# The mLSTM's four projections as seven half-size products instead of eight

## The chip, the cores and the metric

The kernel runs on one NeuronCore of a Trainium2 chip. The metric is the device time of one execution in microseconds (us); lower is better. TensorE (PE) multiplies, VectorE (DVE), ScalarE (ACT) and GpSimd (POOL) do the elementwise work, SyncE (SP) issues most transfers.

## The reference, cut to what matters

A two-layer hybrid encoder step on 256 prompt and 64 sample frames, 320 columns in all, in 32-bit floats, model width 1024. Each layer is

```
h = rms(x, norm_mix)
proj = h @ w_in            # among its columns m_q, m_k, m_v, m_o, 256 wide each, and m_if, 8 wide
y_a: conv + RG-LRU   y_b: latent attention   y_c: retention   y_d: mLSTM(m_q, m_k / 8, m_v, gates from m_if)
x = x + concat(head_rms(y_a), head_rms(y_b), head_rms(y_c), head_rms(y_d) * sigmoid(m_o)) @ w_out
x = x + (silu(g) * u) @ w_down,   g, u = rms(x) @ w_gu
```

The mLSTM part first needs the two gate rows for each head (a running sum of log-sigmoid and a running maximum over the frames), then q, k and v.

## The kernel before

All activations stand transposed in on-chip memory: `hT` is the normalised input, 8 tiles of 128 features by 320 frames. A layer runs through stages whose order is written out by hand, engine by engine, in four functions (`tensor`, `scalar`, `vector`, `gpsimd`); semaphores tie them together. `need(engine, name, ...)` waits for a named result, `step` issues an instruction that announces one (and waits for it on its own engine), `claim(pe, use)` waits until the last user of a PSUM bank has been read, `fill` announces that a bank is full. `layer_uses` lists which of the 8 banks each use has, in order. PE takes its instructions strictly in the order written, so a wait at one of them holds back all that follow.

Weights come in chunks of 256 columns (1 MB) through a ring of 5 slots, loaded by SP in the order ql, kvr, mo, mv, mq, mk, rq and so on; a slot is loaded again when PE has used its last chunk. 

The stage of the change lies between the products of the latent keys (`kvr`, line 891) and the first mLSTM scores (`ds0`, lines 813 to 815). On PE it is: `mo` (two outputs of 128 features, 8 products of 128x128 by 320 columns each, line 785), four transposes of the old state (layer 0 alone, line 901), the gates' transposes `mgt` (907), `mv` (785), `cnT`, `qms` (915, 920), the transposes of the values `mvt0`, `mvt1` (797), the latent queries `qt0` to `qt2` (927), `mq` and `mk` (785), three tiles of attention keys `kv0` to `kv2` (860), the gate rows' transposes `rT` and `gx` (948, 954), the first retention query `rq0` (785), the mLSTM keys' transposes `mkt` (806), and `ds0`. An instruction on 32-bit data shows as two in the profile, so one projection is 32 rows of line 785.

On DVE the stage is a long chain in one order: latent queries (1705, 1706), key copies (1698, 1701), latent sum, then from 1730 the latent keys with their norm (to 1744), the clamp of `mo` (1749), gate rows (1753 to 1757), rotary keys (1760 to 1770), in layer 0 a state table (1683) and the decay-rate table `lam_tables` (1659 to 1677, in the middle of which it waits for an exponential of ACT, line 1384), `lfr` (1776), the copies of the latent queries (1782), the scans and five row operations on 4 partitions (1788 to 1795), the queries' norm and rotation (1800 to 1823), the copies of `mq` (1807), and the key copies of `kv0` to `kv2`. ACT copies `mv` and `mk` out of PSUM (1387, 1416), makes the keys' squares (1354), then the sigmoid of the output gate (1306 to 1308), and copies `gx` (1429), the bank of which `ds0` takes over. POOL only issues transfers in this stage.

The feed-forward part already uses a seven-product form (Strassen's, in Winograd's variant): a 2x2 block product of weight quarters by halves of the 320 columns takes 7 products of 160 columns instead of 8 (line 1133). POOL makes three sums of weight quarters for each chunk (lines 602 to 605, four instructions of 128x512), DVE adds the products up (2104 to 2112).

Of the kernel before, what the change touches and what calls it, by code (L numbers as in the profile page):

```python
# [21 lines left out]
P = 128  # L22
# [39 lines left out]
NQ = KT // 2  # L62
MIXES = FT - 1 + 3 * NQ
MSLOTS = 3
# [60 lines left out]
def layer_uses():  # L125
# [9 lines left out]
    d("ql0", "ql1", "kvr", "mo0", "mo1", "mgt", "mv0", "mv1")  # L135
    u += [("cnT", (4,)), ("qms", (5,))]
    d("mvt0", "mvt1")
    u += [("qt0", (6,)), ("qt1", (7,)), ("qt2", (2,))]
    d("mq0", "mq1", "mk0", "mk1")
# [52 lines left out]
LAST_USE = {"kvr": "kvr", "ql": "ql1", "mo": "mo1", "mv": "mv1", "mq": "mq1", "mk": "mk1", "rq": "rq1",  # L192
# [6 lines left out]
def build(nc, I, O):  # L199
    with ExitStack() as ctx:  # L200
# [120 lines left out]
        gate = part(2, T)  # L321
        dmx = part(512)
        dh = part(2, 512)
        wt = part(2, 576)
        vw = part(2, NT, HD + 1)
        qg = part(H, P)
        ytm = part(NT, H, HD)
# [7 lines left out]
        xgm = mixT  # L335
        dhf = dh[:, :, :].rearrange("p a n -> p (a n)")
# [248 lines left out]
        def _(pool):  # L585
            step = stepper(pool, "pool_chain")

            def mix_weights(l, i):
# [8 lines left out]
                if i == 1:  # L597
                    need(pool, "h_sums", l, 4)
# [27 lines left out]
            for l in range(DEPTH):  # L626

                if l == 0:
# [15 lines left out]
                    pool.dma_start(cst[:, c1:], I["consts"][:, c1:]).then_inc(sem("tables_loaded"), 16)  # L644
                need(pool, "ckv_new", l, 1)
# [4 lines left out]
                out(O["s_krope"][l, 0], krr[0:DEC, 2, :])  # L650
                need(pool, "m_rows", l, 1)
# [5 lines left out]
                out(O["s_mm"][l].rearrange("b h -> h b"), mro[:, T - 1:T])  # L657
                need(pool, "q_ready", l, 1)
# [70 lines left out]
        def _(pe):  # L729
# [58 lines left out]

            def value_tiles(which, l, p):
# [3 lines left out]
                need(pe, "v_raw", l, 4, (0 if which == "mv" else 2) + p + 1)  # L793
# [60 lines left out]
            for l in range(DEPTH):  # L854
# [39 lines left out]
                for p in range(2):  # L894
                    feature(f"mo{p}", l, "mo", p * P, P)
                if l == 0:
# [6 lines left out]
                    ins.then_inc(sem("rows_turned"), 1)  # L903
                claim(pe, "mgt", l)
# [4 lines left out]
                for p in range(2):  # L909
                    feature(f"mv{p}", l, "mv", p * P, P)  # L910
# [11 lines left out]
                for p in range(2):  # L922
                    value_tiles("mv", l, p)
                for t in range(NT):
# [4 lines left out]
                    fill(ins, f"qt{t}")  # L929
                if l == 0:  # L930
# [3 lines left out]
                for p in range(2):  # L934
                    feature(f"mq{p}", l, "mq", p * P, P)
                for p in range(2):
                    feature(f"mk{p}", l, "mk", p * P, P)
# [5 lines left out]
                if l == 0:  # L943
                    pe.wait_ge(sem("ct_ready"), 1)
# [14 lines left out]
                need(pe, "mq_ready", l, 2)  # L959
# [163 lines left out]
                def product(use, l, i, p, right, opens, closes):  # L1123
# [3 lines left out]
                    if p in (3, 5, 6, 7):  # L1127
                        need(pe, "mixed", l, MIXES, i + 1)
# [36 lines left out]
                def hidden_units(j):  # L1165
# [11 lines left out]
                    def h_sum(n, made_n):  # L1177
                        def right(k):
                            if j == 1 and k == 0:
                                need(pe, "h_sums", l, 4, made_n)  # L1180
# [104 lines left out]
        def _(act):  # L1285
# [49 lines left out]
            for l in range(DEPTH):  # L1335
# [40 lines left out]

                if l == 0:
# [4 lines left out]
                if l == 0:  # L1382
                    act.wait_ge(sem("lam"), 1)
                    A(lamt[:, 1, :], lamt[:, 0, :], ACT.Exp, scale=-1.0).then_inc(sem("lam_exp"), 1)
# [12 lines left out]
                for p in range(2):  # L1397
                    value_raw(f"mv{p}", p)
# [5 lines left out]
                for p in range(2):  # L1404
                    value_copy("mv", "d", p)
# [3 lines left out]
                       qtm[:, :, :, :].rearrange("p t h e -> p (t h e)"), ACT.Square), "q_stats")  # L1409
                need(act, "q_ms", l, 1)  # L1410
# [798 lines left out]
```

## Time and profile before

| | |
|---|---|
| median of 3 runs | 928.33 us (928.27 to 928.68) |
| the profiled execution's own time | 928.3 us |
| its span, first to last instruction | 926.5 us |
| PE, DVE, ACT, POOL busy | 920.3, 498.6, 209.9, 444.4 us |
| granted TensorE clock, mean | 1.000 |

The profile is that of one execution. Busy time of PE includes modelled ends of matmuls, so near 100% says that there was always one in flight, not that it went at its peak. The time lies 1.8 us above the span.

### The profile page before, as it was taken

Reading aid. Unit: us, or ns where it says so; the run is one execution under the profiler, and the core shown is the slowest. Engines: PE = TensorE matmul, PEld = TensorE weight load, DVE = VectorE, ACT = ScalarE, POOL = GpSimd, SP = SyncE. Lnnn points to the kernel's source line nnn. Section 1 sums busy time; section 2 is a strip of 40 time slices with the busy share of each in tenths; the row PEclk is TensorE's granted clock in tenths of the full one; section 3 lists DMA queues with packets and bytes.
Section 4 is the critical chain, followed back from the end, with each engine's and each line's share of the span. In section 5 each row is a group of like instructions: output and inputs, shape, how many; then the busy total and the mean of one; then the engine's idle time right before and its main releaser. Section 6 shows DMA issues by size and latency. Waiting matters only on the chain.

```text
span 926.5 us, 14897 instructions
## 1 busy us (share of the span) xinstructions
PE 920.3 (99%) x5712; PEld 812.7 (88%) x5712; DVE 498.6 (54%) x1018; ACT 209.9 (23%) x457; POOL 444.4 (48%) x469
## 2 busy tenths in 40 slices
PE   8999999999999999999999999999999999999998
PEld 6777877778999999999977678777799999999998
DVE  6674656845565656512363665577356556563221
ACT  3224255432000000100132244462310011100001
POOL 6210380125966666676411215403268666666670
PEclk9999999999999999999999999999999999999999
DMA  9969312129555554433434673112655555533321
GB/s 280 237 131 98 112 46 92 52 17 251 138 139 141 142 141 144 134 129 126 133 124 136 30 147 96 47 48 50 138 150 141 143 142 143 147 125 126 131 94 39
DMA packets 159636, 113.02 MB, mean 122 GB/s; under 512 B 10247, under 2 KB 157357, under 8 KB 159437
## 3 DMA queue, kind: packets, MB, share of 16 engines
q1 hardware_dynamic: 154660, 104.50, 39.0%
q0 software_dynamic: 4272, 6.80, 7.3%
q8 instruction: 46, 0.75, 0.3%
q10 hardware_dynamic: 632, 0.75, 0.3%
q14 instruction: 26, 0.21, 0.1%
HBM read 108.46 MB, written 2.27 MB: 120 GB/s over the span
## 4 chain that ended last, share of the span: by engine, by line
PE 98%; DMA 1%; ACT 0%; SPq 0%; DVE 0%; issue 0%; DVEq 0%; ACTq 0%
PE ps L1133 52%; PE ps L785 20%; PE ps L1090 8%; PE ps L1151 2%; PE ps L891 1%; PE ps L860 1%; PE ps L987 1%; PE ps L927 1%; PE ps L1028 1%; PE ps L1037 1%; PE ps L813 1%; PE ps L833 1%; PE ps L970 1%; DMA arena<-in_x_sample 1%; PE ps L1048 1%; PE ps L1069 0%
## 5 line engine op out<-in xcount | busy, mean ns | idle before, releaser
L785 PE MATMUL ps<-hT,ring 128*128 128x320 f32 x608 | 169.4, 434 | 0.3 <-DVEq L433 0.3
L602 POOL TENSOR_TENSOR work<-ring 128x512 f32<-128x512 f32 (+1 forms) x66 | 81.8, 1239 | 153.7 <-issue 113.4
L785 PEld LDWEIGHTS ps<-hT,ring 128*128 128x128 f32 x608 | 113.7, 190 | 45.6 <-DVEq L433 0.8
L1133 PE MATMUL ps<-mixT,ring 128*128 128x160 f32 x672 | 105.0, 299 | 0.0
L1133 PE MATMUL ps<-hT,work 128*128 128x160 f32 x672 | 98.5, 299 | 0.0
L1133 PE MATMUL ps<-hT,ring 128*128 128x160 f32 x672 | 98.1, 299 | 0.0
L1133 PEld LDWEIGHTS ps<-mixT,ring 128*128 128x128 f32 x672 | 95.8, 190 | 0.0
L1133 PEld LDWEIGHTS ps<-hT,ring 128*128 128x128 f32 x672 | 93.7, 190 | 0.3
L1133 PEld LDWEIGHTS ps<-hT,work 128*128 128x128 f32 x672 | 93.7, 190 | 0.0
L604 POOL TENSOR_TENSOR work<-ring 128x512 f32<-128x512 f32 (+1 forms) x66 | 82.4, 1248 | 5.2
L603 POOL TENSOR_TENSOR ring<-ring 128x512 f32<-128x512 f32 (+1 forms) x66 | 82.2, 1246 | 5.2
L605 POOL TENSOR_TENSOR work<-ring,work 128x512 f32<-128x512 f32 (+1 forms) x66 | 81.9, 1242 | 5.2
L1562 ACT ACTIVATE arena<-ps 128x160 f32<-128x160 f32 x42 | 12.8, 304 | 286.8 <-PE ps L1133 286.8
L1090 PE MATMUL ps<-mixT,ring 128*128 128x320 f32 x256 | 71.1, 434 | 0.0
L2142 DVE TENSOR_TENSOR arena<-arena,ps 128x160 f32<-128x160 f32 x8 | 2.6, 321 | 118.6 <-ACT arena L1580 118.6
L1090 PEld LDWEIGHTS ps<-mixT,ring 128*128 128x128 f32 x256 | 48.0, 190 | 19.3
L1133 PE MATMUL ps<-work,ring 128*128 128x160 f32 x352 | 55.6, 299 | 0.0
L1133 PE MATMUL ps<-mixT,work 128*128 128x160 f32 x336 | 52.5, 299 | 0.0
L1133 PE MATMUL ps<-arena,work 128*128 128x160 f32 x352 | 51.7, 299 | 0.0
L1133 PEld LDWEIGHTS ps<-work,ring 128*128 128x128 f32 x352 | 50.4, 190 | 0.0
L1133 PEld LDWEIGHTS ps<-arena,work 128*128 128x128 f32 x352 | 49.1, 190 | 0.0
L1133 PE MATMUL ps<-arena,ring 128*128 128x160 f32 x330 | 48.7, 299 | 0.0
(398 smaller groups left out, 1389.9 us busy)
## 6 DMA issues: line engine op xcount, KB each, us to landing
ring<-in_w_gu SPq DMA_DIRECT2D x88, 512.0 KB, 5.2
ring<-in_w_in SPq DMA_DIRECT2D x44, 512.0 KB, 7.2
ring<-in_w_down SPq DMA_DIRECT2D x32, 512.0 KB, 4.4
ring<-in_w_out SPq DMA_DIRECT2D x16, 512.0 KB, 4.4
ring<-in_w_down SPq DMA_DIRECT2D x16, 384.0 KB, 3.4
cst<-in_consts POOLq DMA_DIRECT2D x1, 1664.0 KB, 12.2
ring<-in_w_in SPq DMA_DIRECT2D x2, 640.0 KB, 5.5
arena<-r POOLq DMA_DIRECT2D x8, 160.0 KB, 17.4
```

Source lines behind the costliest of these rows:

```text
L602: step(tt(s3, a11, a21, ALU.subtract))
L603: step(tt(a21, a21, a22, ALU.add))
L604: step(tt(s2, a21, a11, ALU.subtract))
L605: step(tt(s4, a12, s2, ALU.subtract), "mixed")
L785: ins = mm(bank(use, 0, T, m), w[:, k, c:c + m], right[:, k, 0:T], start=(k == 0), stop=(k == KT - 1))
L813: mm(bank(use, 0, 256), k[:, 0:128], q[:, 0:256], start=True, stop=True)
L833: ins = mm(bank(use, 200 + 64 * s, 64, e), a, b_, start=(t == tiles[0]), stop=(t == tiles[-1]))
L860: fill(mm(bank(f"kv{i}", 0, 512), lat, wkvb[:, :], start=True, stop=True), f"kv{i}")
L1090: ins = mm(bank(u, 0, T), w[:, k, (n % 2) * P:(n % 2 + 1) * P], mixT[:, k, :], start=(k == 6), stop=(k == 5), skip_group_check=True)
L1133: ins = mm(bank(use, at * HT, HT), left, right(k), start=(opens and k == 0 and at == 0), stop=(closes and k == n - 1), skip_group_check=True)
L1151: return mm(bank(use, 0, T), w[:, k, q * P:(q + 1) * P], xg[:, k, :], start=(k == 0), stop=(k == KT - 1))
L1562: step(A(p1c[:, j % 2, :], bank(f"fa{j}", 0, HT), ACT.Copy), "p1_copied")
```

## The change

Each of the four projections mo, mv, mq, mk becomes one `feature_pair` of seven products of 4 x (128x128 by 160 columns). Products that need only raw weights come first (1, 2, 4), then those with sums. Four half sums of `hT` are made once a layer by DVE (`half_sums`, after the latent queries), three sums of weight quarters for each projection by POOL (`pair_weights`, four instructions of 128x512), ACT copies the first product (`pair_first`), DVE combines the rest (`pair_result`, five instructions, for mo a clamp more). The results go to on-chip memory; ACT then copies queries and keys to their places. In DVE's order the scans move ahead of the copies of the latent queries, `state_tables` ahead of mo's result, and `lam_tables` behind mq's result. In PE's order the latent queries move ahead of the values' transposes, which now wait for mv's result. On POOL the sums stand among its transfers: mo and mv first, mq behind the four transfers of the latent keys, mk behind the broadcasts of the gate rows.

```
+    u += [("moa", (2,)), ("mob", (6,)), ("moc", (1,)), ("mgt", (0,)), ("mva", (5,)), ("mvb", (7,)), ("mvc", (4,))]
+    u += [("cnT", (6,)), ("qms", (0,)), ("qt0", (1,)), ("qt1", (2,)), ("qt2", (6,)), ("mvt0", (5,)), ("mvt1", (7,))]
+    u += [("mqa", (4,)), ("mqb", (0,)), ("mqc", (3,)), ("mka", (1,)), ("mkb", (2,)), ("mkc", (7,))]
 ...
     u += [("rT", (3,)), ("gx", (2,)), ("mkt", (6, 7))]
 # gpsimd
+            def pair_weights(l, i):
+                s2, s3, s4 = (pair_sums[i % 2][:, s] for s in range(3))
+                if i < 2:
+                    wait_filled(pool, ("ql1", "kvr")[i], l)
+                    if l == 0 and i == 1:
+                        pool.wait_ge(sem("rows_turned"), 3)
+                else:
+                    wait_used(pool, PAIRS[i - 2], l)
+                wait_chunk(pool, name, l)
+                step(tt(s3, a11, a21, ALU.subtract))
+                step(tt(a21, a21, a22, ALU.add))
+                step(tt(s2, a21, a11, ALU.subtract))
+                step(tt(s4, a12, s2, ALU.subtract), "mixed")
...
+                for i in range(2):
+                    pair_weights(l, i)
                 need(pool, "ckv_new", l, 1)
 ...
                 out(O["s_krope"][l, 0], krr[0:DEC, 2, :])
+                pair_weights(l, 2)
                 need(pool, "m_rows", l, 1)
 ...
                 out(O["s_mm"][l].rearrange("b h -> h b"), mro[:, T - 1:T])
+                pair_weights(l, 3)
                 need(pool, "q_ready", l, 1)
 # tensor
+            def feature_pair(name, l):
 ...
+                claim(pe, a, l)
+                one(a, 0, lambda k: w[:, k, 0, 0, :], half(0, 0), True)
+                one(a, 2, lambda k: w[:, k, 1, 0, :], half(1, 0))
+                claim(pe, c, l)
+                one(c, 1, lambda k: w[:, k, 1, 1, :], half_sum(4), True)
+                claim(pe, b_, l)
+                need(pe, "mixed", l, MADE, i + 1)
+                one(b_, 0, lambda k: w[:, k, 0, 1, :], half_sum(1), True)
+                fill(one(b_, 1, lambda k: s3[:, k, :], half_sum(2)), b_)
+                fill(one(a, 1, lambda k: s2[:, k, :], half_sum(3)), a)
+                fill(one(c, 0, lambda k: s4[:, k, :], half(1, 1)), c)
 ...
-                for p in range(2):
-                    feature(f"mo{p}", l, "mo", p * P, P)
+                feature_pair("mo", l)      # and so for mv, mq, mk
 ...
-                need(pe, "v_raw", l, 4, ...)
+                    need(pe, "pair_made", l, NPAIR, 2)      # value_tiles("mv")
 # scalar
+                def pair_first(name):
+                    if i > 0:
+                        need(act, "pair_made", l, NPAIR, i)
+                    wait_filled(act, f"{name}a", l)
+                    step(A(pair_p1, bank(f"{name}a", 0, HT), ACT.Copy), "p1_copied")
 ...
+                pair_first("mq")
+                need(act, "pair_made", l, NPAIR, 3)
+                for n in range(4):
+                    step(A(qh[rs, n, :], raw[rs, n // 2, :], ACT.Copy), "mq_ready")
+                pair_first("mk")
+                if l == 0:
+                    act.wait_ge(sem("lam"), 1)
+                    A(lamt[:, 1, :], lamt[:, 0, :], ACT.Exp, scale=-1.0).then_inc(sem("lam_exp"), 1)
+                key_stats(range(3), KTILES - 3)
+                need(act, "pair_made", l, NPAIR, 4)
                 for p in range(2):
+                    step(A(kf[:, p, 0:T], raw[:, 2 + p, :], ACT.Copy, scale=0.125), "mk_ready")
 # vector
+                def half_sums():
+                    step(v.tensor_tensor(hp[:, 0], h_at(0, 1), h_at(0, 0), ALU.subtract), "h_sums")
+                    step(v.tensor_tensor(hp[:, 1], h_at(1, 1), h_at(0, 1), ALU.subtract), "h_sums")
+                    step(v.tensor_tensor(hp[:, 2], h_at(1, 1), hp[:, 0], ALU.subtract), "h_sums")
+                    step(v.tensor_tensor(hp[:, 3], h_at(1, 0), hp[:, 2], ALU.subtract), "h_sums")
+                def pair_result(name):
+                    need(dve, "p1_copied", l, P1S, PAIRS.index(name) + 1)
+                    step(v.tensor_tensor(u2, p1, bank(a, HT, HT), ALU.add))
+                    step(v.tensor_tensor(c11, p1, bank(a, 2 * HT, HT), ALU.add), bank_read=(a, l))
+                    wait_filled(dve, b_, l)
+                    step(v.tensor_tensor(halves(u34), halves(bank(b_, 0, T)), u2..., ALU.add))
+                    step(v.tensor_tensor(c22, u34[:, HT:T], bank(b_, 0, HT), ALU.add), bank_read=(b_, l))
+                    wait_filled(dve, c, l)
+                    step(v.tensor_tensor(mid, halves(u34), halves(bank(c, 0, T)), ALU.add), "pair_made")
+                    # mo: then max(SIG_MIN) over 128x640, "pair_made"
 ...
                 query_latents(1)
+                half_sums()
 ...
+                if l == 0:
+                    state_tables()
+                pair_result("mo")
 ...
-                if l == 0:
-                    state_tables()
-                    lam_tables()
 ...
+                scans()
+                pair_result("mv")
                 need(dve, "qlat_rstd", l, 1)     # then the copies of the latent queries
 ...
+                pair_result("mq")
+                if l == 0:
+                    lam_tables()
+                pair_result("mk")
                 key_copies(range(3), KTILES - 3)
```

## Rows read from the trace of the kernel before

**Rows 1.** The page's first part: busy us, share of the span, instructions.
```profile
PE 920.3 (99%) x5712; PEld 812.7 (88%) x5712; DVE 498.6 (54%) x1018; ACT 209.9 (23%) x457; POOL 444.4 (48%) x469
```
**Rows 2.** The chain that ended last, in order: start us, us, what.
```profile
33.58 8.61 PE ps L785 x32
...
52.61 0.71 PE ps L797 x6
...
57.20 17.23 PE ps L785 x64
...
77.68 0.50 PE ps L954 x4
...
83.34 0.43 PE ps L813 x2
...
223.10 237.71 PE ps L1133 x1750
...
487.53 8.63 PE ps L785 x32
...
537.28 0.43 PE ps L813 x2
```
**Rows 3.** The DVE timeline: start us, us, engine, line, operation, tiles, shapes, count.
```profile
25.43 0.55 DVE L1706 SCALAR_TENSOR_TENSOR arena<-ps,cols,rstd 128x320 f32<-128x320 f32 x1
...
33.69 0.18 DVE L1730 COPY mift<-ps 128x24 f32<-128x24 f32 x1 [0.62 <-PE ps L891]
...
38.15 0.56 DVE L1744 TENSOR_TENSOR arena<-arena,bcn 128x384 f32<-128x384 f32 x1
...
58.07 0.68 DVE L1788 TENSOR_TENSOR_SCAN work<-cst,work 4x256 f32<-4x256 f32 x1
...
61.74 0.31 DVE L1795 TENSOR_SCALAR nm<-mro 4x320 f32<-4x320 f32 x1
...
76.23 0.42 DVE L1698 COPY arena<-ps 128x256 f32<-128x256 f32 x1 [4.92 <-ACT arena L1354]
...
221.99 0.83 DVE L2084 TENSOR_TENSOR mixT<-hT 128x640 f32<-128x640 f32 x1 [0.18 <-DVE hT L2077]
...
484.29 0.55 DVE L1706 SCALAR_TENSOR_TENSOR arena<-ps,cols,rstd 128x320 f32<-128x320 f32 x1
```
**Rows 4.** DVE's groups by line and form, 223 to 400 us: busy, mean ns, idle.
```profile
L2125 DVE TENSOR_TENSOR arena<-arena 128x160 f32<-128x160 f32 x11 | 14.1, 1282 | 0.4
...
L2107 DVE TENSOR_TENSOR arena<-ps,arena 128x320 f32<-128x320 f32 x21 | 10.3, 492 | 11.4 <-PE ps L1133 11.0
...
L2105 DVE TENSOR_TENSOR arena<-arena,ps 128x160 f32<-128x160 f32 x21 | 6.7, 321 | 0.8
```
**Rows 5.** POOL's groups by line and form, whole span.
```profile
L602 POOL TENSOR_TENSOR work<-ring 128x512 f32<-128x512 f32 x58 | 73.8, 1272 | 146.8 <-issue 108.8 <-DMA ring<-in_w_gu 21.5 <-DVE mixT L2087 15.9
```
**Rows 6.** The POOL timeline: four copies on 32 partitions, twice.
```profile
569.67 2.14 POOL L674 COPY work<-work 32x320 f32<-32x320 f32 x4 [1.29 <-DMA out_s_mn<-sst]
...
576.24 1.98 POOL L674 COPY work<-work 32x320 f32<-32x320 f32 x4
```
**Rows 7.** The POOL timeline around the stage of layer 0: its transfers.
```profile
27.52 0.66 POOL L644 DMA_DIRECT2D cst<-in_consts  x1
...
46.77 0.73 POOL L613 DMA_DIRECT2D out_p_krope<-arena  x1 [6.48 <-DVE arena L1770]
```
**Rows 8.** The DVE timeline: the decay-rate table after its wait, first and last.
```profile
47.81 0.23 DVE L1665 TENSOR_SCALAR lamt<-lamt 128x4 f32<-128x4 f32 x1
...
52.43 0.17 DVE L1677 TENSOR_SCALAR c<-lamt 128x4 f32<-128x4 f32 x1
```
**Rows 9.** The ACT timeline, 74 to 83 us.
```profile
74.46 0.44 ACT L1416 ACTIVATE work<-ps 128x320 f32<-128x320 f32 x1 [3.80 <-PE ps L785]
...
82.51 0.28 ACT L1429 ACTIVATE glb<-ps 128x132 f32<-128x132 f32 x1
```
**Rows 10.** The PE timeline: 24 products of 128 columns, the first of the execution.
```profile
1.07 4.92 PE L738 MATMUL ps<-work 128*128 128x128 f32 x24 [1.07 <-DVE work L1595]
```

More of the change, by code:

```diff
@@ L62 @@
 NQ = KT // 2
+PAIRS = ("mo", "mv", "mq", "mk")
+NPAIR = len(PAIRS)
 MIXES = FT - 1 + 3 * NQ
+MADE = NPAIR + MIXES
+P1S = NPAIR + FT - 1 + NQ
 MSLOTS = 3
@@ L326, in build @@
         qg = part(H, P)
+        ytm_at = wk
         ytm = part(NT, H, HD)
@@ L787, in feature, with one, half, half_sum @@
                     fill(ins, use)
+            def feature_pair(name, l):
+                i = PAIRS.index(name)
+                w, _ = quarters(name, l)
+                s2, s3, s4 = (pair_sums[i % 2][:, s] for s in range(3))
+                a, b_, c = f"{name}a", f"{name}b", f"{name}c"
+                def one(use, at, left, right, opens=False):
+                    for k in range(KT // 2):
+                        ins = mm(bank(use, at * HT, HT), left(k), right(k), start=(opens and k == 0),
+                                 stop=(k == KT // 2 - 1), skip_group_check=True)
+                    return ins
+                def half(jj, t):
+                    return lambda k: hT[:, 2 * k + jj, t * HT:(t + 1) * HT]
+                def half_sum(n):
+                    if i == 0:
+                        need(pe, "h_sums", l, 8, n)
+                    return lambda k: hp[:, n - 1, k, :]
+                wait_chunk(pe, name, l)
+                claim(pe, a, l)
[9 more added lines that the diff above has]
+                fill(one(c, 0, lambda k: s4[:, k, :], half(1, 1)), c)
             def value_tiles(which, l, p):
@@ L792, in value_tiles @@
                 claim(pe, u, l)
-                need(pe, "v_raw", l, 4, (0 if which == "mv" else 2) + p + 1)
+                if which == "mv":
+                    need(pe, "pair_made", l, NPAIR, 2)
+                else:
+                    need(pe, "v_raw", l, 2, p + 1)
                 if which == "rv":
@@ L908, in _ @@
                 fill(ins, "mgt")
-                for p in range(2):
-                    feature(f"mv{p}", l, "mv", p * P, P)
+                feature_pair("mv", l)
                 claim(pe, "cnT", l)
@@ L921, in _ @@
                 fill(ins, "qms")
-                for p in range(2):
-                    value_tiles("mv", l, p)
                 for t in range(NT):
@@ L929, in _ @@
                     fill(ins, f"qt{t}")
+                for p in range(2):
+                    value_tiles("mv", l, p)
                 if l == 0:
@@ L933, in _ @@
                     pe.wait_ge(sem("consts_loaded"), 16 * 5)
[L934 to L937, printed above, removed]
+                    pe.wait_ge(sem("ct_ready"), 1)
+                feature_pair("mq", l)
+                feature_pair("mk", l)
                 need(pe, "ckvT", l, 1)
@@ L1395, in value_copy @@
                     now_read(act, u)
-                for p in range(2):
-                    value_raw(f"mv{p}", p)
+                pair_first("mv")
                 wait_filled(act, "cnT", l)
@@ L1409, in _ @@
                        qtm[:, :, :, :].rearrange("p t h e -> p (t h e)"), ACT.Square), "q_stats")
+                for p in range(2):
+                    value_copy("mv", "d", p)
                 need(act, "q_ms", l, 1)
@@ L1745, in _ @@
                                      bcn[:, l, 0:KVR].unsqueeze(1).broadcast_to([P, NT, KVR]), ALU.mult), "ckv_new")
-                for p in range(2):
-                    wait_filled(dve, f"mo{p}", l)
-                    step(v.tensor_scalar(gate[:, p, :], bank(f"mo{p}", 0, T), SIG_MIN, None, ALU.max), "gate_arg")
-                    now_read(dve, f"mo{p}")
+                if l == 0:
+                    state_tables()
+                pair_result("mo")
                 wait_filled(dve, "mgt", l)
```

99 lines of the change are left out of this document (56 added, 43 removed).

## The prediction

> **What bounds the kernel now.** I read the page's busy times first: PE is busy in all but 6 us of the span, POOL and DVE in about half of it [rows 1]. Then the chain that ended last, in order of time: in the stage of the change it is PE alone, from one group to the next without a gap [rows 2]. So here a microsecond less of PE work is a microsecond gained, but only if every result that PE asks for is there in time; the timelines of DVE and POOL say how much room there is [rows 3, 7]. The page's share of busy time hides this: DVE looks half idle over the span, while in this stage it works nearly without pause.
>
> **What PE saves.** The pair mq and mk takes 17.23 us as 64 rows, so a projection 8.62 us. In the feed-forward part 1750 rows of 160 columns take 237.71 us, 0.1358 us each [rows 2]. Seven products of four matmuls are 56 rows: 7.61 us. That is 1.01 us for each of eight projections, 8.1 us together, if PE never waits. Nothing else on PE grows: the other groups stay, in another order.
>
> **What DVE gets.** By kind: a difference over 128x640 takes 0.83 us [rows 3], a sum with one operand in PSUM 0.32 us for 160 columns and 0.49 us for 320 [rows 4]. With the 0.03 us between instructions, the half sums are 3.4 us, a projection's result 0.32 + 0.32 + 0.49 + 0.32 + 0.49 = 1.94, with gaps 2.1 us, and mo's clamp over 640 elements at most 0.8. What they replace (the clamp and the copies out of PSUM, 0.5 us each for 320 columns) is about as long, so DVE's list grows by the half sums and little more; but now PE waits at the middle of it: the transposes of the values come only after the last instruction of mv's result, and ahead of that stand the whole of mo's result, the gate rows, the rotary keys and the scans.
>
> **POOL beside DVE, where I part from the plain sum.** In the feed-forward part a DVE difference of 128x160 with both operands in on-chip memory takes 1.28 us on average, the same size with one operand in PSUM 0.32 [rows 4]. POOL's weight sums take 1.27 us each at that time [rows 5]. So a DVE instruction that reads two operands from on-chip memory stands until the POOL instruction in flight ends: 0.96 us more each. PSUM operands free it from this. It doesn't depend on the number of partitions, on POOL's side at least: four copies on 32 partitions took 2.14 us beside DVE's work and 1.98 otherwise [rows 6]. The Trainium skill (SBUF — State Buffer, Who interferes with whom) has the same rule, a DVE instruction with two SBUF inputs against a GpSimd one that reads SBUF, as an exclusive lock held for a whole instruction; the trace agrees. Without that rule the sum below would end 13 us lower, before any loss by the clock. POOL had only transfers to issue in this stage [rows 7]; now it gets 4 x 1.27 us and gaps, 5.4 us, four times a layer.
>
> **DVE's chain, layer 0.** The last latent query ends at 25.98 [rows 3]. Half sums to 29.4; POOL's last early transfer ends at 28.2 [rows 7], mo's sums follow at once, so one half sum is held: 30.3. The key copies of the four past tiles, waiting on ACT in turn, took 26.83 to 32.09, so they end at 35.3; the latent sum, one operation held by POOL, at 37.2. The latent keys' work, which began at 33.69 because PE was done then [rows 3], begins 3.5 us later; one of its squares meets mv's sums (0.96), so its end, before at 38.71, is at 43.1. Then state table 0.7, mo's result 2.1 and clamp 0.8: 46.8; three gate rows 1.6; seven rotary operations 1.85; lfr 0.5: 50.8. The nine scans and row operations take 58.07 to 62.05, 4.0 us [rows 3]. POOL takes mq's sums 1.4 us after the rotary keys (two transfers of which the first takes 0.73 [rows 7]), so they fall on the scans: four of the nine are held, by 3.9 us. Scans end at 58.7, mv's result at 60.8. PE would be there much earlier: between 33.58 and 57.20 it has 23.6 us, less 0.7 for the six transposes [rows 2], less 2 x 1.01: at 54.4. It stands for 6.4 us.
>
> From there: transposes 0.7, mq and mk 15.2, then the 8.9 us that lie between 74.43 and ds0 at 83.34 [rows 2]: ds0 at 85.7 without another wait. Two more come in layer 0. DVE begins the decay-rate table ahead of mk's result, but the exponential that it waits for stands on ACT behind the copy of mk's first product, at 76.3. From there its 4.8 us [rows 8] and the four operations that read mk's bank, 1.6 us, end at 82.8; gx, 3.1 us behind mk's end at 76.8, wants that bank: 3.0 us. And ds0 waits for ACT to read gx: from DVE's first key copy to that read it took 76.23 to 82.79 [rows 3, 9], 6.6 us, now with the two key copies of 0.44 [rows 9], moved ahead of the sigmoid, and their gaps 7.5. The first copy is at 83.3, so ds0 at 90.8, another 2.1 us. Against 83.34 layer 0 loses 7.4 us.
>
> **Layer 1.** Half sums begin at 484.84 [rows 3], with POOL on mo's sums from 480.8: held twice, 490.1. The latent sum, held 0.6, ends at 491.6, where PE was done at 487.5 + 0.1; one held square, then as above without tables: latent keys 497.5, mo 500.5, gate rows 502.1, rotary keys 503.9, lfr 504.5, scans and 3.9 us held 512.4, mv's result 514.5. PE would be there at 507.9: 6.6 us. No table stands ahead of mk's result, so gx does not wait; ds0 follows at 514.5 + 0.7 + 15.2 + 8.9 = 539.3, and ACT's longer list adds 0.3: 539.7 against 537.28 [rows 2], 2.4 us lost. Both together 9.9 us. Behind ds0 DVE, ACT and PE keep their distances, PE is the bound again, and nothing is given back.
>
> POOL itself is in time: mo's sums end at 34.2 and are wanted at 37.3, mq's end 8 us and mk's 6 us ahead. I cost them at nothing. If POOL were late by more, PE would wait in the middle of a projection instead.
>
> **The clock.** PE never paused for over 1.3 us after its start. Its first 24 products of 128 columns, after a pause of 1.07 us and whatever came before, take 4.92 us, 0.205 each [rows 10]; by 0.1358 for 160 columns they would take about 0.109 each, an estimate, 2.6 us in all. The level of 1.2 GHz is my reading of the factor of 1.9. After a pause of 6.5 us the bounds are nothing and another such stretch, 2.3 us lost. I take the upper end for each layer, since a start after no work at all is the nearest row: 4.6 us. The Trainium skill (TensorE: Matmul & The Clock Gate, HAM oscillation — how this bites in real kernels) warns of falls of the clock in PE's pauses; no pause of the kernel before is long enough to show it.
>
> **The sum.** 928.3 us is the profiled execution's own time, within 0.03 of the median. 928.3 + 7.4 + 2.4 + 4.6 = 942.8, about 942.7 us.
>
> **Rivals.**
> 1. As above but the clock stays up: 928.3 + 9.9 = 938.2. The pauses may be too short, and the column of the granted clock shows full speed even in the slow first stretch, so the trace can't decide.
> 2. Scans and operations on 4 partitions are not held by POOL: no row shows either beside POOL's work. Then 3.9 us fall away in each layer, the rest being held or hidden: layer 0 loses 5.0, layer 1 gains 0.2: 933.1. The clock would stay up after pauses of 4 us, or cost up to 4 more.
> 3. Faster: nothing on DVE is held in this stage, since POOL's reads and DVE's here fall in different memory or the waits interleave better. The place is the values' transposes; mv's result would end at 53.9 and 507.4, where PE needs it at 54.4 and 507.9. It decides at 0.5 us of delay, from which on every microsecond is lost. Layer 1 gains 4.2, layer 0 still loses 0.9 by the two waits at mk: 925.0. Rows 4 speak strongly against it.
> 4. POOL is held so much by DVE that it is late for the products, or the clock stays down through the waits at mk in layer 0: 946 or more.
>
> **Chances and range.** Forecast 0.45, rival 1 0.22, rival 2 0.15, rival 3 0.10, the rest 0.08. Range 931.5 to 945.5, which leaves out rival 3 and the dearest cases. Faster, same and slower are parted at 0.2% (1.9 us), about what a measurement tells from no change. Faster 0.10, same 0.04 (a mixture of rivals 2 and 3 near 928), slower 0.86.
>
> **What the profile after would show.** PE: 56 rows for a projection in 7.6 us; a pause of some 6 us before the values' transposes (line 797's form with `work`) in each layer, ended by DVE; in layer 0 alone 3 us before gx and 2 us before ds0. DVE: four scans or row operations at 1.2 to 1.5 us instead of 0.3 to 0.5, half sums partly at 1.8. The granted clock below 1 behind the pauses. Wrong I am if the scans keep their lengths beside POOL's sums, if POOL's sums of mq come after the scans, or if the clock does not fall.

## The result, and the profile after

The changed kernel takes 946.13 us (median of 4 runs, 945.49 to 947.39), the kernel before 928.50 beside it: 1.0189 times as long, with a 95% interval of 1.0172 to 1.0207. The profiled execution took 945.51 us, its span 943.7. The forecast was 942.7 with a range up to 945.5. The sign and the hold came as forecast; the loss was put 3.4 us too low, and the measured time lies 0.6 us above the range. The trace explains 2.8 of the 3.4 us, since the profiled execution was 0.6 us faster than the median. Of all the executions below one stands apart, at 1363.86 us and a granted clock of 0.654 (one of ten without POOL's sums); the intervals leave it out.

The waits of PE, in the changed kernel (what waited, for whom; us in total, times, the longest). Before, PE had no such wait in either of these stages [rows 2]:

```profile
PE ps L872 <- DVE work L1823: 12.7, 2, 7.5
PE ps L1022 <- DVE work L1817: 3.0, 1, 3.0
PE ps L836 <- DVE mixT L1798: 1.9, 1, 1.9
PE ps L888 <- ACTq L448: 0.6, 1, 0.6
```

L872 are the transposes of the values, which wait in each layer for the last instruction of mv's result (L1823). L1022 is gx, which waits for mk's result. Both were forecast, at 6.4 and 6.6 us and at 3.0 us. The third, within mo's products of layer 1, was not.

PE's timeline in layer 0, same kernel (start, us, what; in brackets the pause ahead of it):

```profile
61.93 1.51 PE L872 MATMUL ps<-cst,work 128*128 128x128 f32 x6 [7.50 <-DVE work L1823]
63.23 3.67 PE L836 MATMUL ps<-hT,ring 128*128 128x160 f32 x16
...
72.18 2.34 PE L836 MATMUL ps<-hT,ring 128*128 128x160 f32 x16
...
85.98 0.38 PE L1022 MATMUL ps<-r,cst 4*128 4x4 f32 x2 [3.00 <-DVE work L1817]
...
87.07 7.62 PE L823 MATMUL ps<-hT,ring 128*128 128x320 f32 x16
...
95.18 0.60 PE L888 MATMUL ps<-work 128*128 128x256 f32 x2
```

Sixteen rows take 3.67 us behind the first pause and 2.34 further on, and rq0, 4.58 us before, takes 7.62 behind the second pause. So a pause is paid twice: once as idle time, once as slow products behind it. ds0 (L888) starts at 95.18; on the same timeline of the kernel before it started at 83.18 (the chain in [rows 2] counts it from 83.34). The stretches of the same time (start and end in us, length, busy time of each engine, then the granted clock, DMA):

```profile
59.00:61.00 2.00, 0.00 (x0) 0.00 (x0) 1.79 (x7) 0.00 (x0) 0.72 (x2) 0.53 0.00 0
61.00:63.00 2.00, 1.07 (x5) 1.10 (x6) 1.71 (x4) 0.00 (x0) 1.86 (x4) 0.50 1.35 41
65.00:67.00 2.00, 2.00 (x13) 2.00 (x12) 1.51 (x2) 1.38 (x4) 1.90 (x2) 0.76 0.36 10
...
89.00:91.00 2.00, 2.00 (x6) 1.22 (x5) 0.87 (x3) 1.79 (x4) 0.00 (x0) 0.50 1.09 349
```

0.50 is the lower of the clock's two levels, 1.2 GHz, held while PE is fully busy from 87 to 93 us.

Why the result is late stands on DVE's timeline, the scans of layer 0 (before, with the row operations, 58.07 to 62.05 us [rows 3]):

```profile
51.34 0.68 DVE L1829 TENSOR_TENSOR_SCAN work<-cst,work 4x256 f32<-4x256 f32 x1
52.05 2.15 DVE L1831 TENSOR_TENSOR_SCAN mro<-work 4x256 f32<-4x256 f32 x1
54.23 1.17 DVE L1829 TENSOR_TENSOR_SCAN work<-cst,work 4x64 f32<-4x64 f32 x1
55.44 1.30 DVE L1831 TENSOR_TENSOR_SCAN mro<-work,m 4x64 f32<-4x64 f32 x1
56.78 1.51 DVE L1832 TENSOR_TENSOR r<-work 4x320 f32<-4x320 f32 x1
58.32 0.48 DVE L1833 TENSOR_TENSOR r<-work,mro 4x320 f32<-4x320 f32 x1
```

POOL's timeline at the same time:

```profile
52.38 1.28 POOL L617 TENSOR_TENSOR work<-ring 128x512 f32<-128x512 f32 x1
53.73 1.53 POOL L618 TENSOR_TENSOR ring<-ring 128x512 f32<-128x512 f32 x1
55.34 1.26 POOL L619 TENSOR_TENSOR work<-ring 128x512 f32<-128x512 f32 x1
56.68 1.26 POOL L620 TENSOR_TENSOR work<-ring,work 128x512 f32<-128x512 f32 x1
```

Four DVE instructions end 0.1 to 0.5 us behind the POOL instruction that they met: 54.20 behind 53.66, 55.40 behind 55.26, 56.74 behind 56.60, 58.29 behind 57.94. That lag is what each takes alone (0.68, 0.28, 0.34 and 0.48 us, in the run without POOL's sums) less 0.1 to 0.2 us: by these rows a held instruction does nearly all its work behind POOL's. The recorded start does not tell who is held: the first of the four began 0.33 us ahead of POOL's sum. The 4.0 us of scans and row operations became 8.3. The half sums of layer 1 are held likewise, three of four by 1.0 us each:

```profile
496.97 1.84 DVE L1795 TENSOR_TENSOR mixT<-hT 128x640 f32<-128x640 f32 x1
498.85 0.82 DVE L1796 TENSOR_TENSOR mixT<-hT 128x640 f32<-128x640 f32 x1
499.71 1.91 DVE L1797 TENSOR_TENSOR mixT<-hT,mixT 128x640 f32<-128x640 f32 x1
501.65 1.77 DVE L1798 TENSOR_TENSOR mixT<-hT,mixT 128x640 f32<-128x640 f32 x1
```

The last ends at 503.42, and mo's third product (PE at 501.7 without a wait) reads it: 1.86 us of waiting. In all, layer 0 added 12.0 us by the start of its feed-forward part (223.10 us before, 235.10 after), and layer 1 another 5.1 by its ds0 (537.12 and 554.26 on the timelines).

### The profile page after: what moved, and what is told of

Same layout as the page of the kernel before. It is cut to its first block, busy times and chain, and to the rows that moved or that the text cites. A ratio compares the mean times of both kernels' runs of the same rounds, so it can differ in the third digit from the quotient of the medians.

```text
span 943.7 us, 15398 instructions
## 1 busy us (share of the span) xinstructions
PE 919.4 (97%) x5904; PEld 830.3 (88%) x5904; DVE 533.8 (57%) x1056; ACT 214.4 (23%) x469; POOL 486.0 (51%) x501
## 4 chain that ended last, share of the span: by engine, by line
PE 88%; DVE 9%; ACT 2%; issue 1%; POOL 0%; DVEq 0%; ACTq 0%; POOLq 0%
PE ps L1203 51%; PE ps L823 11%; PE ps L1160 7%; PE ps L836 3%; PE ps L1221 2%; PE ps L1057 1%; PE ps L1098 1%; PE ps L888 1%; PE ps L1107 1%; DVE mro L1831 1%; PE ps L908 1%; PE ps L1040 1%; PE ps L1118 1%; DVE hT L1693 0%; PE ps L1139 0%
## 5 line engine op out<-in xcount | busy, mean ns | idle before, releaser
L823 PE MATMUL ps<-hT,ring 128*128 128x320 f32 x352 | 102.4, 445 | 0.0
L1203 PEld LDWEIGHTS ps<-hT,ring 128*128 128x128 f32 x672 | 93.7, 190 | 0.3
L823 PEld LDWEIGHTS ps<-hT,ring 128*128 128x128 f32 x352 | 67.2, 195 | 26.2 <-issue 2.2
L1160 PEld LDWEIGHTS ps<-mixT,ring 128*128 128x128 f32 x256 | 48.1, 190 | 19.2
```

What stands on the lines that cost most here:

```text
L823: ins = mm(bank(use, 0, T, m), w[:, k, c:c + m], right[:, k, 0:T], start=(k == 0), stop=(k == KT - 1))
L1160: ins = mm(bank(u, 0, T), w[:, k, (n % 2) * P:(n % 2 + 1) * P], mixT[:, k, :], start=(k == 6), stop=(k == 5), skip_group_check=True)
L1203: ins = mm(bank(use, at * HT, HT), left, right(k), start=(opens and k == 0 and at == 0), stop=(closes and k == n - 1), skip_group_check=True)
```

## The experiments

The theory: POOL's weight sums hold DVE's instructions with two on-chip operands, so the results that PE now waits for are late, and each pause costs clock besides. The rivals: DVE's own longer list does it; the order of the work does it; the clock is another matter. All kernels are the changed one with the edit shown, unless "before" is said; the edits are cut to what matters, and as each adds or removes lines, one instruction's line number differs by a few from kernel to kernel. Times are medians, and 928.4 to 928.5 us is the kernel before measured beside them.

**POOL's sums left out.**

```
-                step(tt(s3, a11, a21, ALU.subtract))
-                step(tt(a21, a21, a22, ALU.add))
-                step(tt(s2, a21, a11, ALU.subtract))
-                step(tt(s4, a12, s2, ALU.subtract), "mixed")
+                step(nc.gpsimd.memset(s4[:, 0, 0:1], 0.0), "mixed")
...
-                fill(one(b_, 1, lambda k: s3[:, k, :], half_sum(2)), b_)
+                fill(one(b_, 1, lambda k: w[:, k, 0, 0, :], half_sum(2)), b_)
```

The other two products with sums read raw quarters likewise.

> The changed kernel (946.1 us) with POOL's four weight sums of each mLSTM projection left out; the products that read them read the raw weight quarters instead, so the instructions of PE, DVE and ACT stay the same in number and shape, and the mLSTM's values are wrong. Theory (POOL's sums hold DVE's two-operand instructions): the three held half sums fall from 1.8 to about 0.83 us, the scans L1829-1836 lose their 1.5 us, PE's wait of 1.9 us for half sum 4 in layer 1 goes, the pause at the values' transposes shrinks from 7.5 to 2.5-4 us in layer 0 and from 5.2 to 2-3.5 in layer 1; the 3.0 us wait behind the decay-rate table stays. With some of the clock loss this gives 932-938 us. Rival (DVE's own longer list makes the result late, POOL is no cause): durations on DVE as before, pauses 7 and 5 us, 944 us or more.

Measured: 926.89 us, 0.9982 of before (0.9972 to 0.9991), 19.2 us less than the changed kernel and 5 us below the expected range: I had left the holds only 8 to 14 us, and pauses of 2 to 4 us that did not come. Between 33 and 100 us PE has one wait:

```profile
PE ps L1019 <- DVE work L1814: 3.0, 1, 3.0
```

and DVE's scans have their old lengths:

```profile
48.49 0.68 DVE L1826 TENSOR_TENSOR_SCAN work<-cst,work 4x256 f32<-4x256 f32 x1
49.20 0.68 DVE L1828 TENSOR_TENSOR_SCAN mro<-work 4x256 f32<-4x256 f32 x1
```

With the same instructions on DVE, mv's result is there 7.2 us earlier (54.6 instead of 61.8), 0.1 us before PE comes to it, and both pauses at the values' transposes are gone. The list is not too long; it is held. The wait behind the table is there without POOL too, so it has a cause of its own.

**The sums for mq behind the scans.**

```
-                pair_weights(l, 2)
                 need(pool, "m_rows", l, 1)
+                pair_weights(l, 2)
```

> One move: POOL makes the sums for mq behind the scans instead of beside them. Theory: the scans of both layers fall from 5.5 to 4.0 us, the values' result ends 1.5 us earlier, the pauses are 6.0 and 3.7 us, the sums (ready near 64 us) are still in time for PE (66 us): 942.5-943.5 us. Rival (scans over 4 partitions take that long beside any POOL work, or the hold is not the cause): 945.5-946.5 us, unchanged. Second rival (mk's sums, now 5 us later, are late for PE): a new wait of 1-3 us at mk, 945-948 us.

Measured: 941.77 us, 4.4 us less. That is 0.7 us below the expected range. The scans and row operations took 4.0 us again and the pauses at the values fell to 3.5 and 0.9 us, by 4.0 and 4.3. My expectation counted the hold of one scan instead of four instructions; the prediction's own figure of 3.9 us was the right one. The gain was not twice 4: the clock fell behind the pause of 3.5 us as it had behind that of 7.5, and in layer 1 POOL was now late for mk by 1.2 us and ACT for ds0 by 2.3.

**The table's exponential earlier.** ACT's exponential and the three DVE instructions that feed it go behind the query statistics.

```
+                if l == 0:
+                    act.wait_ge(sem("lam"), 1)
+                    A(lamt[:, 1, :], lamt[:, 0, :], ACT.Exp, scale=-1.0).then_inc(sem("lam_exp"), 1)
                 pair_first("mq")
...
                 pair_first("mk")
-                if l == 0:
-                    act.wait_ge(sem("lam"), 1)
-                    A(lamt[:, 1, :], lamt[:, 0, :], ACT.Exp, scale=-1.0).then_inc(sem("lam_exp"), 1)
```

> Only the decay-rate table's exponential on ACT is moved from behind mk's first product to behind the query statistics, with the three DVE instructions that feed it; the table's other 22 instructions stay between the results of mq and mk but no longer wait (idle 3.9 us before L1747). Theory: the result of mk ends 4 us earlier, PE's 3.0 us wait for the gx bank goes, the clock does not fall there, so rq0 takes 4.5 us instead of 7.5; a wait of 1-2 us at ds0 (ACT's chain) comes back: 940.5-942.5 us. Rival (the clock falls there on account of the first pause, not of this one): gain 3 us at most less the ds0 wait, 943-945 us.

Measured: 941.26 us, 4.9 us less, as forecast. PE's timeline shows gx without a wait, rq0 back at full speed, and the wait for ACT at ds0 that the faster stretch uncovers:

```profile
83.62 0.36 PE L1022 MATMUL ps<-r,cst 4*128 4x4 f32 x2
...
84.41 4.57 PE L823 MATMUL ps<-hT,ring 128*128 128x320 f32 x16
...
90.93 0.67 PE L888 MATMUL ps<-work 128*128 128x256 f32 x2 [1.29 <-ACTq L448]
```

The first pause stayed at 7.6 us, so the second fall of the clock belonged to the second pause.

**mv's result ahead of the scans.**

```
+                pair_result("mv")
                 need(dve, "kvr_gif_done", l, 2, 2)
...
                 scans()
-                pair_result("mv")
```

> One move on DVE: the result of mv is put together ahead of the scans and the log-sigmoid instead of behind them. Theory (what is late is this result, by the instructions ahead of it): the pause at the values' transposes goes in both layers with its clock loss (about 10.4 and 8 us of time), but mq's and mk's products then reach their own dependencies earlier: query copies (bank 1 and 2) and POOL's sums for mk, so waits of some us come up at mk and again at gx behind the table, since DVE's chain to mk's result has not become shorter: 934-940 us. Rival (the pause itself only hides a later wait of equal size): 944-947 us.

Measured: 942.35 us, 3.8 us less, worse than I expected. The profiled execution was the slowest of the four (944.84 us; the others took 942.14 to 942.43). The pauses at the values are gone in both layers, yet in layer 0 two others stand in their place: 4.2 us for POOL's sums for mk, made only behind the scans and the row copies, and 4.35 us at gx for mk's result, still behind the table; in layer 1 it is 2.4 us for the sums for mk, and 1.8 at ds0 for ACT.

PE's timeline there:

```profile
70.94 1.77 PE L836 MATMUL ps<-mixT,ring 128*128 128x160 f32 x8 [4.18 <-POOL work L620]
72.51 3.60 PE L836 MATMUL ps<-mixT,work 128*128 128x160 f32 x16
...
84.59 0.58 PE L1022 MATMUL ps<-r,cst 4*128 4x4 f32 x2 [4.35 <-DVE work L1817]
...
86.05 7.58 PE L823 MATMUL ps<-hT,ring 128*128 128x320 f32 x16
```

One removed pause uncovers the next dependency, which lay hidden in it.

**PE kept busy in the pause.** Products whose result nobody reads, to part the idle time from the clock.

```
+                if l == 0:
+                    pe.wait_ge(sem("ct_ready"), 1)
+                claim(pe, "mqc", l)
+                for _ in range((13, 9)[l]):
+                    mm(bank("mqc", 0, T), ident, hT[:, 0, 0:T], start=True, stop=True)
                 for p in range(2):
                     value_tiles("mv", l, p)
```

> The changed kernel (946.1 us) with idle matmuls (identity by 128x320, into a bank that is free) put in front of the values' transposes: 13 in layer 0, 9 in layer 1, some 0.54 us each, about as long as the pauses. They compute nothing that is used. Theory (the clock falls because PE stands still, and the fall costs PE time on the chain to the decay-rate table): granted clock 1.00 behind both pauses, transposes 0.8 instead of 1.5 us, mq and mk 15.2 us instead of 16.5 and 16.0; 2.0 us less in layer 0, 1.4 us less in layer 1, the second fall at the gx wait stays: 942.5-943.5 us. Rival (the fall is not from PE's idling, or what it costs is hidden behind DVE's and ACT's chain to ds0 anyway): 945.5-946.5 us.

Measured: 942.26 us, 3.9 us less, though PE was given more work. In the stretch where the changed kernel showed 0.53 and 0.50 the granted clock is 1.00, and the transposes take 0.84 us, the first 16 rows of mq 2.34:

```profile
61.00:63.00 2.00, 1.35 (x10) 0.95 (x9) 1.68 (x5) 0.00 (x0) 1.86 (x5) 1.00 1.35 41
63.00:65.00 2.00, 2.00 (x17) 2.00 (x16) 1.04 (x2) 0.77 (x1) 1.98 (x3) 1.00 0.92 26
...
87.00:89.00 2.00, 2.00 (x5) 1.35 (x4) 1.20 (x3) 1.46 (x4) 0.00 (x0) 0.50 1.09 376
```

Behind the gx wait, which was left alone, it falls as before (last row). So the clock's price at the first pause is real, and for both layers about what this run's expectation had put down: 3.4 us expected, 3.9 measured by the medians and 3.4 between the profiled executions (945.51 and 942.13).

**The sums alone, on the kernel before.** 16 sums per layer into a spare tile, at about the same places; they read `hT` instead of the weights.

```
+                step(tt(s, a11, a21, ALU.subtract))
+                step(tt(s, a21, a22, ALU.add))
+                step(tt(s, a21, a11, ALU.subtract))
+                step(tt(s, a12, s, ALU.subtract))
```

> The kernel BEFORE (928.5 us), unchanged but that POOL makes 16 sums of 128x512 per layer, like those of the change in number, size and place (two sets behind the ql and kvr products, one behind the key rope, one behind the scans), into a spare tile that nobody reads. Theory (the hold lengthens DVE's list by some 6-9 us per layer, and only Strassen's results make PE wait for that list; before, DVE idles 1-5 us at a time in this stretch and PE waits for ACT's copies, not for DVE): scans and half of DVE's two-operand instructions are longer, the time is 928.3-930.5 us. Rival (holds cost time by themselves, as DVE's work is on the chain in either kernel): 934-942 us.

Measured: 928.79 us, 1.0004 of before (0.9995 to 1.0014): no difference. DVE is held there too. POOL's sums run from 48.66 to 54.0 us, and meet the table:

```profile
50.41 0.90 DVE L1687 TENSOR_TENSOR lamt<-lamt 128x4 f32<-128x4 f32 x1
...
51.66 1.00 DVE L1691 TENSOR_TENSOR lamt<-lamt 128x4 f32<-128x4 f32 x1
52.69 0.17 DVE L1692 TENSOR_SCALAR lamt<-lamt 128x4 f32<-128x4 f32 x1
52.90 1.11 DVE L1691 TENSOR_TENSOR lamt<-lamt 128x4 f32<-128x4 f32 x1
...
54.25 0.16 DVE L1691 TENSOR_TENSOR lamt<-lamt 128x4 f32<-128x4 f32 x1
```

A product of 128x4 takes 0.9 to 1.1 us instead of 0.16. (The TENSOR_SCALAR between keeps its 0.17, but it began in the 0.08 us between two of POOL's sums.) The scans, which I had expected to be longer, stand behind this set of sums here, from 59.84 us, and keep 0.68 us. But PE waits for nothing of DVE's in this stage for more than 0.3 us. The hold costs nothing by itself; it costs once the change puts DVE's list on PE's path.

**The orders mended.** DVE: mv's result ahead of the scans, mq's ahead of the query normalisation. POOL: the sums for mq and mk together, ahead of the row copies. The exponential early as above, and the rest of the table far behind, in the chunk attention. Two of these moves:

```
                 pair_weights(l, 2)
+                pair_weights(l, 3)
                 need(pool, "m_rows", l, 1)
...
                 maxima(1)
+                if l == 0:
+                    lam_tables()
                 need(dve, "gate_d", l, 1)
```

> The changed kernel with its orders mended, nothing left out: the result of mv ahead of the scans, POOL's sums for mq and mk both ahead of the gate-row copies, the result of mq ahead of the query normalisation and that of mk behind it, the table's exponential behind the query statistics and the rest of the table in the chunk attention. Theory (every pause was a result or a sum made late, and the sum of work on DVE and POOL fits beside PE): no wait over 1.5 us on PE in front of ds0 but the 1.9 us for half sum 4 in layer 1, clock 1.00 throughout, and most of the 4 us of PE work that the products save per layer is kept: 920-926 us. Rival (DVE with the holds is too slow for PE in any order, the pause only moves on): 930-942 us.

Measured: 946.89 us, a miss by over 20 us. The stage itself had come out better, with ds0 at 86.3 us instead of 95.2, though waits of 2.2 us for the copies of the latent queries and of 2.3 us at ds0 stood in it, where I had expected none over 1.5. But the table's new place was a bad one:

PE's timeline, and a piece of the table on DVE's:

```profile
134.76 0.90 PE L872 MATMUL ps<-cst,work 128*128 128x128 f32 x3 [7.46 <-DVEq L448]
```

```profile
127.62 0.17 DVE L1758 TENSOR_SCALAR lamt<-lamt 128x4 f32<-128x4 f32 x1
127.82 0.70 DVE L1757 TENSOR_TENSOR lamt<-lamt 128x4 f32<-128x4 f32 x1
```

POOL's rope of the retention queries holds its products at 0.70 us here, so it lasts 7.9 us (125.6 to 133.5), and PE's transposes of rv need the banks that DVE reads only behind it. DVE's long idle gap is the next one, ahead of the third maxima.

**The half sums too.** The reordered kernel, and besides: in layer 1 POOL's first set starts behind the normalisation, the second waits for the half sums; in layer 0 two key copies go ahead.

```
+                if l > 0 and i == 0:
+                    need(pool, "normed", l, KT)
+                elif i < 2:
                     wait_filled(pool, ("ql1", "kvr")[i], l)
+                    if i == 1:
+                        need(pool, "h_sums", l, 8, 4)
```

> As the reordered kernel before it in this list, and: in layer 1 POOL's first set of sums starts behind the normalisation instead of behind the ql products, the second set waits for the half sums, and in layer 0 two of the four key copies go ahead of the half sums. Theory: the half sums are held for 0-1 us instead of 3, PE's wait of 1.9 us for half sum 4 in layer 1 goes: 1.5-3 us less than the reordered kernel. Rival (the normalisation or query latents are held instead, or the sums for mv come late): the same or up to 2 us more.

Measured: 944.61 us (943.35 to 946.46), 2.3 us less than the run before it (946.00 to 948.09), with the 1.9 us wait for half sum 4 gone; the two sets of times overlap a little.

**The table ahead of the third maxima,** where DVE idles 6.5 us in the changed kernel.

```
                 queries(2)
+                if l == 0:
+                    lam_tables()
                 maxima(2)
```

> The reordered kernel with mended half sums (944.6 us), in which the rest of the decay-rate table stands in front of the third reading of the maxima instead of in front of the gated output. Its trace shows PE waiting 7.8 us at the transposes of rv behind that table (whose 128x4 products take 0.7 us beside POOL's rope instead of 0.16); DVE idles 6.5 us in front of the third maxima in the changed kernel. Theory: the wait goes, with the clock loss behind it: 933-937 us. Rival (the wait at rv's transposes comes from the pad or another result, the table only stood before it): 943 us or more.

Measured: 935.68 us, 8.9 us less, in the range expected.

**All orders.** Besides, the output gate's sigmoid moves behind the second head's decays, and the query copies ahead of the scans.

```
-                sigmoid(gate[:, :, :].rearrange("p t n -> p (t n)"), one_c[:, :], "gate_d")
                 need(act, "k_ms", l, KTILES)
...
+                    if h == 1:
+                        sigmoid(gate[:, :, :].rearrange("p t n -> p (t n)"), one_c[:, :], "gate_d")
...
                 now_made(dve, "q_copied")
+                rest_of_gates()
```

> The kernel of the run before it, and two more moves: the output gate's sigmoid (three ACT instructions, 2.3 us) stands behind the second head's decays instead of in front of the key statistics, and the copies of the query latents' products stand ahead of the log-sigmoid and the scans. Theory: the waits of 2.3 us at ds0 in both layers go with the clock loss that follows them (the first product behind takes 5.8 instead of 4.5 us), and the 2.2 us wait for the copies in mk's pair of layer 0: with the run before it at 935 this is 925-929 us, about the kernel before. Rival (the holds of DVE's instructions still make some result late, now a later one): 930-934 us.

Measured: 926.33 us, 0.9978 of before (0.9968 to 0.9987), in the range expected. The waits of 2.3 us at ds0 in both layers and of 2.2 us for the copies are gone. One wait of size is left, for mk's result, again with a slow stretch behind it:

```profile
77.28 0.38 PE L1026 MATMUL ps<-r,cst 4*128 4x4 f32 x2 [2.38 <-DVE work L1826]
```

**The sigmoid's move alone, on the kernel before.**

> The kernel BEFORE (928.5 us) with the output gate's sigmoid moved behind the second head's decays, nothing else. It shows what of that move is worth without Strassen's form. Theory: PE waits there 0.6 us at most in front of ds0, so 927.9-928.6 us. Rival (the sigmoid holds up ACT's chain in this kernel too): 925-927 us.

Measured: 928.33 us, 0.9997 of before (0.9988 to 1.0007). The move is worth nothing there, where PE has no such wait at ds0; in the run above the wait of 2.3 us that it removed had come with Strassen's form. The two moves of that run were not tried apart, and of all the moves this is the only one tried on the kernel before.

**mk's result ahead of the queries' rope.**

```
+                pair_result("mk")
+                key_copies(range(3), KTILES - 3)
                 c2, sn, lo, hi = rope_t(None, None, True)
...
-                pair_result("mk")
-                key_copies(range(3), KTILES - 3)
```

> The kernel with all orders mended (926.3 us), and one more move on DVE: the result of mk and the key copies stand ahead of the queries' rope (five instructions, 2.0 us) instead of behind it. Its trace shows mk's last product at 71.7 us, DVE's rope until 75.6, mk's result until 77.8, PE waiting 2.4 us for it at the gx bank and the clock down behind that. Theory: the wait goes (under 1 us is left), the clock stays, ds0 then waits for ACT's chain at most 1-2 us: 922.5-925 us. Rival (the rope is late next, for the query transposes or POOL's clears, or ACT's chain sets ds0 anyway): 925.5-927.5 us.

Measured: 921.52 us (5 runs, 921.20 to 921.86), 0.9920 of before (0.9907 to 0.9934), 24.6 us less than the changed kernel with the same sums and products, and 1 us below the expected range. What PE waits for over its whole span, the start included:

```profile
PE ps L780 <- DVE work L1682: 1.1, 1, 1.1
PE ps L1111 <- ACTq L448: 0.6, 1, 0.6
...
PE ps L840 <- POOL work L624: 0.4, 1, 0.4
PE ps L1026 <- DVE work L1826: 0.3, 1, 0.3
```

## What the prediction had right, and the step that failed

**PE's saving, right.** At full clock mq starts at 62.77 and mk at 70.37 us in the run with a busy PE: 7.60 us a projection, 7.61 forecast. All eight save 8.1 us; the best order keeps 6.9 of it.

**The hold, right in mechanism and price.** The scans and row operations lost 4.3 us in each layer, 3.9 forecast. That ruled out rival 2 (4 partitions are free of it) and rival 3 (nothing is held); the run without the sums and the one with the sums alone show both halves of the argument. The scans are what shows it for few partitions: the copies that the prediction called on [rows 6] are POOL's own, and 2.14 against 1.98 us says little. The Trainium skill (SBUF — State Buffer, Who interferes with whom) states the rule for two SBUF inputs without regard to the shape; the scans on 4 partitions (2.15 us, 0.68 alone) and the 128x4 products (1.1 us, 0.16 alone) agree.

**The half sums, too few held.** I let one be held in layer 0 and two in layer 1; it was three in each. In layer 0 they ended 1.7 us later than forecast and the scans lost 0.4 us more; the held square that I had put in did not come (0.56 us in both layers, its full speed), so mv's result ended at 61.8 us instead of 60.8. In layer 1, with layer 0's loss taken off, it ended 0.6 us later than forecast. And I costed the half sums at nothing for PE: product 3 of mo reads half sum 4 at once, which the text never asked. The 1.9 us were hardly a loss on top: with the 5.2 us at the transposes they make 7.1, and 6.6 was forecast there.

**The step that failed: the clock's.** I charged one fall per layer, 2.3 us each, at the first pause, and none behind the 3.0 us wait at gx that the forecast itself had put down. The first falls cost 2.0 us in layer 0 and 1.4 in layer 1: from the start of the transposes to the end of mk's products it was 17.9 and 17.3 us, and 15.9 in the run with a busy PE. Behind the gx wait the clock fell a second time: rq0 took 7.6 us instead of 4.6, and with the gate rows the slow stretch cost 3.4 us. The 2.1 us wait at ds0 that I had forecast vanished in it: ds0's row has no wait. The run with the exponential early is the test: without the gx wait rq0 is back at 4.6 us, and the time is 4.9 us less.

Added up for layer 0: PE starts on the values 1.1 us later than forecast, the first fall is 0.3 cheaper, and from mk's end to ds0 it loses 6.5 us where 3.0 and 2.1 had been put. That is 2.2 more than the 9.7 forecast with the clock (7.4 and 2.3), and 12.0 was measured, to within the rounding. Layer 1 lost 5.1 us against 4.7. The range reached only 2.8 us above the forecast, less than the second fall alone. Rival 4, with the clock low at the waits behind mk and 946 or more, comes nearest to what happened, but not by its mechanism: POOL was not late, and the clock was back at 1.00 between the two falls, from 67 to 85 us. Rival 1 fell with the first slow row behind the first pause.

**Points of the list.** A pause of some 6 us in each layer: 7.5 and 5.2. 3 us before gx in layer 0 alone: 3.0. 2 us before ds0: 0, hidden in the slow rq0. Scans at 1.2 to 1.5 us: 1.17 to 2.15. Half sums at 1.8: yes. Clock below 1: yes.

**Not settled.** The first half sum of layer 0 took 1.37 us and ended before the first of POOL's sums is recorded (27.81 us), while POOL issued transfers; without the sums, and with the same transfers, it took 0.82. Whether POOL's record begins late or something else holds was not tried. Nor was the best order tried without POOL's sums, so what the holds still cost there is open. The 0.6 us between the profiled execution and the median are in no trace.

## What to carry to other kernels

An exchange of the bound engine's work for another's is priced by the path between them, not by busy shares: the sums and the holds cost nothing where PE didn't wait for DVE (928.8 against 928.4 us), and 19 us where it did. Before such a change, list for each result that PE will newly ask for what stands ahead of it on its engine, and put it first there; when one pause is removed, read the trace again for the dependency it had hidden. Price every pause twice, at each place where one is forecast: in these traces PE's clock fell behind every pause of 2.4 us or more in the two stages, and behind all but one of those of 2.2 and 2.3.

## What the runs showed of the hardware

- The clock fell to its lower level with pauses of 7.5, 5.2, 4.2, 3.5, 3.0, 2.4 and 2.2 us; behind those of 1.9, 1.3 and 1.2 us the rows kept their full speed within 0.1 us. The length of the pause alone does not decide: one of 1.8 us, at ds0 of layer 1 with mv's result first, was followed by a projection of 6.2 us instead of 4.5, with 0.50 granted from 554 to 556 us. In the reordered kernel a pause of 2.3 us ahead of ds0 left the next projection at 4.5 us in layer 0 and made it 5.8 in layer 1, where the granted clock reads as below. The shorter pause was not the cheaper one: behind 3.5 us the first 16 rows took 4.47 us, behind 7.5 us 3.67.

```profile
553.00:555.00 2.00, 1.94 (x8) 1.70 (x9) 1.49 (x5) 1.57 (x3) 0.00 (x0) 0.64 0.56 15
555.00:557.00 2.00, 2.00 (x5) 1.33 (x4) 0.78 (x2) 0.92 (x3) 0.00 (x0) 0.51 0.90 31
```

- A second tensor operand is not needed for a hold. Of the row operations with POOL's sums beside them, the TENSOR_SCALAR that reads one tensor and a column of scalars (m) took 0.97 us in the reordered kernel instead of 0.24. And the last instruction of the table, one tensor times a constant, on-chip memory to on-chip memory, took 0.72 us instead of 0.17 in the run with mk's result early, inside a POOL instruction from 131.03 to 131.90 us:

```profile
62.84 0.97 DVE L1838 TENSOR_SCALAR r<-r,m 4x64 f32<-4x64 f32 x1
...
131.21 0.72 DVE L1768 TENSOR_SCALAR c<-lamt 128x4 f32<-128x4 f32 x1
```

- Not held inside a POOL sum, in the changed kernel: a copy out of PSUM (0.42 us for 128x256, at 33.47), a reduction (0.42, at 33.92) and a memset (0.17, at 37.35).

- POOL is slowed in turn: its sums beside DVE's half sums took 1.67 to 1.74 us instead of 1.27.
